# Compact 64x64 diagonal blocks and 64-row products in the triangular inverse of a two-block transformer kernel

## The chip, the cores and the metric

The kernel runs on one core of one Trainium2 chip (trn2). Time is device microseconds of one launch. TensorE is called PE in the profile (its weight loads PEld), VectorE DVE, ScalarE ACT, GpSimd POOL and SyncE SP. Everything is computed in fp32; a large product is made of three products of a high and a low part (types fp32r), a small one is a plain fp32 product, which shows as two weight loads and two matmuls.

## The reference

The reference is two transformer blocks over 256 tokens of width 1024. The first has three kinds of attention and a feed-forward layer; the second has a feed-forward layer, a mixer and another feed-forward layer. The change lies in the mixer, in its gated delta branch:

```python
A = jnp.where(strict, jnp.einsum('bhntk,bhnsk->bhnts', kb, k) * Lmat, 0.0)
T = lax.linalg.triangular_solve(eye + A, jnp.broadcast_to(eye, A.shape),
                                left_side=True, lower=True, unit_diagonal=True)
u = jnp.matmul(T, v * beta[..., None])
w = jnp.matmul(T, kb * jnp.exp(gam)[..., None])
```

`T` is the inverse of a unit lower triangular matrix. The kernel works on chunks of 128 tokens, so for every key head there are four 128x128 inverses: two chunks (`i` or `b`) times two value heads (`e`).

## The kernel before

Each engine runs its own program, written out by hand, and the engines meet only at semaphores. The part that matters is the loop over eight key heads of the mixer: `head(0, True, False)`, then `head(i, True, True)` for i = 1 to 7, then `head(8, False, True)`. In pass `i` the large product of head `i` (`gemm`) and the small work of head `i - 1` (`main`) are woven together. On PE the large product is cut into 24 quarters (`quarter(n)`) of 12 matmuls each, and between them stand the small products. Pass 8 has no large product; a few products of a later layer (`early_yh`, placed by the table `EARLY`) stand there as filler.

The inverse is built by doubling. `xi` holds the transposed inverse and `yi` the inverse, each 128 rows by 4 matrices of 128 columns; `nt` holds the negated strictly lower part. `yi` starts as the identity with the 1-wide level filled in (L1586, L1599), and `xi` is its transpose (L2245 on PE, L920 on ACT, which makes `t_ready`). For levels l = 1 to 6:

- `inv_t(l - 1)` (L2149, not for l = 1) transposes `xi` into PSUM with four matmuls, and `y_copy` on ACT (L826) takes the new half of the columns into `yi`.
- `inv_z(l)` multiplies `nt` by half of the columns of `xi`: four products, 128 rows deep and 64 columns wide, by `four` (L2118). `z_copy` on ACT (L813) takes the result into `zi`.
- one quarter, and often a product of the other branch (`level`, L2110, L2108, L2103, whose operands DVE makes in `decayed`, L1425 and L1426, and whose result it takes in `scored`, L1435 to L1442).
- `inv_w(l)` multiplies `yi` by `zi`: again four products by `four` (L2118).
- another quarter, and again perhaps a `level`. Meanwhile `inverse(l)` on DVE (L1455; for level 6 L1460) copies the result under a mask into `xi`; semaphore `xx_ready` releases the next `inv_t` and `inv_z`.

After level 6, `yi` multiplies the values (L2171, then the small chain L1533, L2189, L1545, L2195, L1551, L2207). Later in the pass PE makes the key products of the next head (L2234, semaphore `kq_done`), DVE makes `nt` from them (L1595), `mt` (L1597), the start of `yi` (L1599), two more scalings (L1601), then scans, copies and `w_low(4)`, and goes on into the next pass without a branch in between that matters.

DVE and ACT also prepare the weights of the large product in the same in-order queues. ACT's `split` (L556) takes 1.9 us for each piece of weights and DVE's `w_low` (L960) 2.3 us. `split` waits for PE to finish with the slot. All of this stands in one fixed order on each engine.

PSUM bank use in the inverse: `inv_z` writes bank 3 of `M`, `inv_w` bank 4 (level 6: bank 5), `inv_t` bank 5, `level` bank 0. In pass 8 `early_yh` uses bank 2 of `M` from part 14 on.

Of the kernel before, what the change touches and what calls it, by code (L numbers as in the profile page):

```python
# [13 lines left out]
P = 128  # L14
T = 256
# [67 lines left out]
def emit(nc, ctx, a, out):  # L83
# [132 lines left out]
    zi = grid(mix(4 * P), i=TT, e=2, c=P)  # L216
    vn0, vn1 = (grid(mix(2 * P), e=2, c=P) for _ in range(2))
# [21 lines left out]
    def x_half(i, h):  # L239
        return M[:, 2 * i + h, :].rearrange("p (k t) -> p k t", t=P)  # L240

    def yh_bank(tile):
# [61 lines left out]
    zz_done, zc_ready, ww_done, wt_done, xx_ready, yy_ready, yt_done = (  # L304
        sem(n) for n in ("zz_done", "zc_ready", "ww_done", "wt_done", "xx_ready", "yy_ready", "yt_done"))
# [235 lines left out]
    def _(act):  # L541
# [243 lines left out]
        def head(i, gemm, main):  # L785
# [23 lines left out]
            def z_copy(l):  # L809
                if not main:  # L810
                    return
                act.wait_ge(zz_done, l + (i - 1) * 6)
                nc.scalar.activation(halved(zi.rearrange("p i e c -> p (i e c)"), l, 0), packed(M[:, 3, 0:T], l),  # L813
                                     ACT.Copy).then_inc(zc_ready, 1)
# [7 lines left out]
            def y_copy(l):  # L822
                if not main:
                    return
                act.wait_ge(yt_done, l + (i - 1) * 5)
                nc.scalar.activation(halved(yi.rearrange("p i e c -> p (i e c)"), l, 1), halved(M[:, 5, :], l, 1),  # L826
                                     ACT.Copy).then_inc(yy_ready, 1)

            level_exp(1)
            z_copy(1)  # L830
            if not gemm:
                o_hi(0, GH - 1)
# [13 lines left out]
            z_copy(5)  # L846
            split_j(1)
# [70 lines left out]
            if gemm:  # L918
                act.wait_ge(t_done, i + 1)
                nc.scalar.activation(xi, M[:, 4, :].rearrange("p (i e c) -> p i e c", i=TT, e=2), ACT.Copy).then_inc(t_ready, 1)  # L920
# [32 lines left out]
    def _(dve):  # L953
# [420 lines left out]
        def head(i, gemm, main):  # L1374
# [72 lines left out]
            def inverse(l):  # L1447
                if not main:
                    return
                sz = 1 << l  # L1450
                shape = [P, 4, HD // sz, sz]
                if l < LEVELS - 1:
                    dve.wait_ge(ww_done, l + (i - 1) * 5)
                    dve.sem_inc(waited, 1)
                    v.copy_predicated(halved4(xi, l, 0), halved(lmask_t[:, l, :].bitcast(I32), l, 0).unsqueeze(1).to_broadcast(shape),  # L1455
                                      packed(M[:, 4, 0:T], l).rearrange("p (x n) s -> p x n s", x=4)).then_inc(xx_ready, 1)
                else:
                    dve.wait_ge(wt_done, i)
                    dve.sem_inc(waited, 1)
                    v.copy_predicated(halved4(yi, l, 1), halved(lmask[:, l, :].bitcast(I32), l, 1).unsqueeze(1).to_broadcast(shape),  # L1460
                                      packed(M[:, 5, 0:T], l).rearrange("p (x n) s -> p x n s", x=4)).then_inc(yy_ready, 1)
# [128 lines left out]
            if gemm:  # L1590
                dve.wait_ge(kq_done, i + 1)
                kk = M[:, 2, 0:3 * P].rearrange("p (b c) -> p b c", b=3)
                for e in range(2):
                    for b in range(TT):
                        v.scalar_tensor_tensor(out=nt[:, b, e, :], in0=kk[:, 2 * b, :], scalar=nbst[:, b, e:e + 1],  # L1595
                                               in1=lt[:, e, 2 * P * b:2 * P * b + P], op0=ALU.mult, op1=ALU.mult)
                v.tensor_tensor(mt, kk[:, 1, :].unsqueeze(1).to_broadcast([P, 2, P]), lt[:, :, P:T], ALU.mult)  # L1597
                settle()
                v.copy_predicated(yi, lmask[:, 0, :].bitcast(I32).unsqueeze(1).unsqueeze(1).to_broadcast([P, TT, 2, P]), nt)  # L1599
# [67 lines left out]
    def _(pe):  # L1667
# [397 lines left out]
        def early_yh(n):  # L2065
# [6 lines left out]
        EARLY = {2: (0, 2), 3: (2, 4), 4: (4, 6), 5: (6, 8), 6: (8, 10), 7: (10, 12), 8: (12, 14), 9: (14, 16),  # L2072
                 10: (16, 18), 11: (18, 19), 12: (19, 20), 13: (20, 21)}

        def head(i, gemm, main):
# [38 lines left out]
            def four(out_bank, lhs, rhs, l, side, done):  # L2114
                for b in range(TT):
                    for e in range(2):
                        at = P * b + HD * e
                        ins = mm(packed(M[:, out_bank, at:at + HD], l), lhs[:, b, e, :], halved(rhs[:, b, e, :], l, side),  # L2118
                                 start=True, stop=True)
                ins.then_inc(done, 1)  # L2120

            def inv_z(l):
# [6 lines left out]
                four(3, nt, xi, l, 0, zz_done)  # L2129

            def inv_w(l):
                if not main:
                    return
                pe.wait_ge(zc_ready, l + (i - 1) * 6)
                if l > 1:
                    pe.wait_ge(yy_ready, l - 1 + (i - 1) * 6)
                if l < LEVELS - 1:
                    four(4, yi, zi, l, 0, ww_done)
                else:
                    four(5, zi, yi, l, 1, wt_done)  # L2140

            def inv_t(l):
                if not main or l == 0:
                    return
                pe.wait_ge(xx_ready, l + (i - 1) * 5)
# [7 lines left out]
            for l in range(1, LEVELS):  # L2153
                inv_t(l - 1)
                inv_z(l)
                quarter(2 * l - 2)
# [11 lines left out]
            if main:  # L2168
                pe.wait_ge(yy_ready, i * 6)
# [148 lines left out]
```

## Time and profile before

| | us |
|---|---|
| median of 3 runs (1525.44 to 1526.99) | 1525.87 |
| the profiled execution | 1524.43 |
| its span, first to last instruction | 1522.7 |

| engine | busy us | share of span | instructions |
|---|---|---|---|
| PE | 1481.0 | 97% | 11072 |
| PEld | 1395.2 | 92% | 11072 |
| DVE | 1009.1 | 66% | 1559 |
| ACT | 716.4 | 47% | 960 |
| POOL | 28.7 | 2% | 73 |

The passes 1 to 8 of the head loop lie between about 765 and 1232 us. A busy PE is not a PE at its peak: matmuls overlap, so the length of one record is longer than the distance to the next, and costs have to be read from the distances of starts. DMA moves 148 GB/s on average and is busy half the time. Nothing in the head loop waits for weights to arrive.

### The profile page before, as it was taken

To read this page: it belongs to the slowest core of one execution; us is meant where nothing else is said; L and a number is where in the kernel's file an instruction comes from. 1 tells how busy PE (TensorE), PEld (TensorE's weight loads), DVE (VectorE), ACT (ScalarE), POOL (GpSimd) and SP (SyncE) were. 2 spreads that over 40 slices of the span, in tenths; PEclk is the share of its full clock that TensorE was granted. 3 is DMA by queue.
4 is the path that set the end of the run, shared out by engine and by line. 5 is a ranking of instruction groups with operands and counts; after the bars stand their busy time and mean duration, and the time that the engine had idled before them with its cause. 6 is when DMAs were issued, how large, how long until landed. Compare 5 with 4: busy or idle time off the path is not lost.

```text
span 1522.7 us, 28790 instructions
## 1 busy us (share of the span) xinstructions
PE 1481.0 (97%) x11072; PEld 1395.2 (92%) x11072; DVE 1009.1 (66%) x1559; ACT 716.4 (47%) x960; POOL 28.7 (2%) x73
## 2 busy tenths in 40 slices
PE   8999999999999999999999999999999999999998
PEld 8999999978999799998899999999999899799997
DVE  5786667674555755456888788787787755555544
ACT  4444444644444543445436546455464453444443
POOL 6000000000000000000000000000000000000000
PEclk9999999999999999999999999999999899999999
DMA  8454444555556456654643343443442325566661
GB/s 264 140 167 138 133 127 131 194 189 188 180 189 203 143 177 194 193 174 133 182 114 91 94 125 83 110 110 85 108 105 88 111 72 181 163 194 193 180 194 68
DMA packets 304640, 224.94 MB, mean 148 GB/s; under 512 B 10418, under 2 KB 288068, under 8 KB 304580
## 3 DMA queue, kind: packets, MB, share of 16 engines
q1 hardware_dynamic: 304580, 224.09, 49.5%
q8 instruction: 44, 0.72, 0.2%
q14 instruction: 16, 0.13, 0.0%
HBM read 223.02 MB, written 1.05 MB: 147 GB/s over the span
## 4 chain that ended last, share of the span: by engine, by line
PE 76%; DVE 13%; DVEq 4%; ACT 4%; issue 2%; DMA 0%; ACTq 0%
PE G L1674 15%; PE G L1676 14%; PE G L1675 14%; PE M L1679 5%; PE M L1680 5%; PE M L1681 5%; PE M L2118 4%; DVEq L957 4%; DVE w_lo L960 3%; PE M L1674 2%; PE M L1676 2%; PE M L1675 2%; ACT w_hi L556 2%; PE M L2149 1%; PE M L2110 1%
## 5 line engine op out<-in xcount | busy, mean ns | idle before, releaser
L960 DVE TENSOR_TENSOR w_lo<-w_raw,w_hi 128x2048 fp32r<-128x2048 f32 (+1 forms) x208 | 475.3, 2286 | 241.3 <-ACT w_hi L556 240.1
L1674 PE MATMUL G<-xa_hi,w_hi 128*128 128x256 f32 x2152 | 630.4, 293 | 0.9 <-DVE w_lo L960 0.5
L1675 PE MATMUL G<-xa_lo,w_hi 128*128 128x256 f32 x2152 | 608.8, 283 | 0.0
L1676 PE MATMUL G<-xa_hi,w_lo 128*128 128x256 f32 x2152 | 608.8, 283 | 0.0
L556 ACT ACTIVATE w_hi<-w_raw 128x2048 fp32r<-128x2048 f32 x207 | 395.0, 1908 | 288.4 <-PE G L1676 186.1
L1674 PEld LDWEIGHTS G<-xa_hi,w_hi 128*128 128x128 f32 x2152 | 411.9, 191 | 9.1 <-issue 7.5
L1675 PEld LDWEIGHTS G<-xa_lo,w_hi 128*128 128x128 f32 x2152 | 412.1, 191 | 6.0 <-issue 4.9
L1676 PEld LDWEIGHTS G<-xa_hi,w_lo 128*128 128x128 f32 x2152 | 411.4, 191 | 0.1
L1679 PE MATMUL M<-w_hi,xb_hi 128*128 128x512 f32 x304 | 118.9, 391 | 0.9 <-DVE xb_lo L960 0.9
L1680 PE MATMUL M<-w_lo,xb_hi 128*128 128x512 f32 x304 | 118.7, 390 | 0.0
L1681 PE MATMUL M<-w_hi,xb_lo 128*128 128x512 f32 x304 | 118.3, 389 | 0.0
L2118 PE MATMUL M<-arena 128*128 128x64 f32 x768 | 101.5, 275 | 1.5 <-ACT arena L813 1.4
L2118 PEld LDWEIGHTS M<-arena 128*128 128x128 f32 x768 | 96.1, 196 | 3.0 <-ACT arena L813 3.0
L731 ACT ACTIVATE arena<-G 128x256 f32<-128x256 f32 x44 | 16.9, 384 | 140.7 <-PE G L1676 140.7
L1679 PEld LDWEIGHTS M<-w_hi,xb_hi 128*128 128x128 f32 x304 | 57.2, 188 | 12.2 <-issue 1.4
L1681 PEld LDWEIGHTS M<-w_hi,xb_lo 128*128 128x128 f32 x304 | 57.1, 188 | 12.3
L1680 PEld LDWEIGHTS M<-w_lo,xb_hi 128*128 128x128 f32 x304 | 57.2, 188 | 10.6
L960 DVE TENSOR_TENSOR xb_lo<-arena,xb_hi 128x256 fp32r<-128x256 f32 (+2 forms) x68 | 35.3, 519 | 34.5 <-ACT xb_hi L733 21.2
L1291 DVE TENSOR_TENSOR arena<-arena,G 128x256 f32<-128x256 f32 x44 | 18.5, 421 | 56.7 <-ACT arena L731 56.7
L826 ACT ACTIVATE arena<-M 128x256 f32<-128x256 f32 x40 | 15.7, 392 | 85.2 <-PE M L2149 85.2
L1455 DVE COPY_PREDICATED arena<-lmask_t,M 128x256 f32<-128x256 int32 x40 | 24.4, 611 | 34.6 <-PE M L2118 32.7
L1384 DVE SCALAR_TENSOR_TENSOR arena<-arena 128x256 f32<-128x256 f32 x96 | 42.0, 479 | 2.2
(352 smaller groups left out, 2002.9 us busy)
## 6 DMA issues: line engine op xcount, KB each, us to landing
w_raw<-in_w_in SPq DMA_DIRECT2D x166, 512.0 KB, 4.5
w_raw<-in_ffn_w_in SPq DMA_DIRECT2D x88, 512.0 KB, 4.9
w_raw<-in_w_ff SPq DMA_DIRECT2D x64, 512.0 KB, 4.2
w_raw<-in_ffn_w_out SPq DMA_DIRECT2D x44, 512.0 KB, 4.0
w_raw<-in_w_out SPq DMA_DIRECT2D x16, 512.0 KB, 4.2
w_raw<-in_w_branch_gdn SPq DMA_DIRECT2D x16, 512.0 KB, 5.1
w_raw<-in_w_branch SPq DMA_DIRECT2D x12, 512.0 KB, 4.3
w_raw<-in_w_branch_hgrn SPq DMA_DIRECT2D x8, 512.0 KB, 3.9
```

The lines of the kernel that those rows point to most:

```text
L556: nc.scalar.activation(w_hi[:, slot, :], w_raw[:, slot, :], ACT.Copy).then_inc(hi_ready, 1)
L957: v.drain()
L960: return v.tensor_tensor(dst, src, hi.bitcast(F32), ALU.subtract)
L1384: ins = v.scalar_tensor_tensor(out=acc[:, n, :], in0=x, scalar=w, in1=acc[:, n, :], op0=ALU.mult, op1=ALU.add)
L1455: v.copy_predicated(halved4(xi, l, 0), halved(lmask_t[:, l, :].bitcast(I32), l, 0).unsqueeze(1).to_broadcast(shape), packed(M[:, 4, 0:T], ...
L1674: mm(out_, w[0], x[0], start=first, stop=False)
L1675: mm(out_, w[0], x[1], start=False, stop=False)
L1676: return mm(out_, w[1], x[0], start=False, stop=last_)
L1679: mm(out_, x[0], w[0], start=first, stop=False)
L1680: mm(out_, x[0], w[1], start=False, stop=False)
L1681: return mm(out_, x[1], w[0], start=False, stop=last_)
L2118: ins = mm(packed(M[:, out_bank, at:at + HD], l), lhs[:, b, e, :], halved(rhs[:, b, e, :], l, side), start=True, stop=True)
```

## The change

The level loop keeps the 64x64 diagonal blocks in compact form until level 5. A new tile `xc` holds, on its lower 64 partitions, the upper left block of each of the four transposed inverses, and on its upper 64 partitions the lower right block; so it is 256 columns wide instead of 512. `yc` and `zc` are compact views of the memory of `yi` and `zi`. `ntq` is a view of `nt` in another column order, so that the 64 columns of a block of both value heads lie side by side.

- `inv_z(l)` for l = 1 to 5 makes four products of 64 rows, one for each chunk and each half of the array (partitions 0 to 63 and 64 to 127), with 128 weight columns and 64 moving columns. The two halves write banks 3 and 4.
- `inv_w(l)` for l = 1 to 5 makes four products of 64 rows, one for each chunk and value head, again alternating between the halves. They write banks 1, 2, 3 and 4, 64 columns each.
- For level 6 both are four products of 64 rows, 64 weight columns and 64 moving columns, all on the same quarter of the array.
- `inv_t(l)` for l = 0 to 4 is two transposes of 128x128 instead of four; `inv_t(0)` is new and stands behind `inv_z(1)`. `inv_t(5)` is four as before.
- ACT has a new `y_copy(0)` of 256 columns behind `z_copy(1)`; `y_copy` copies 128 columns for l = 1 to 4 and 512 for l = 5. `spread` is new: two copies of 64 partitions take `xc` into `xi` behind `z_copy(5)` (semaphore `xf_ready`, awaited by DVE's `inverse(5)`). The copy L920 becomes two copies of 64 partitions.
- DVE's `inverse(l)` for l = 1 to 5 is two masked copies of 64 partitions and 128 columns instead of one of 128 partitions and 256 columns. For level 6 it is an unmasked copy of 64 partitions. Two memsets of 64 partitions stand ahead of the wait for `kq_done`, and the masked copy that starts `yi` is cut in two.
- `EARLY` moves filler in pass 8 from quarters 8 and 9 to quarters 10 to 12.

Its core:

```diff
+    xc = grid(mix(2 * P), i=TT, e=2, c=HD)
+    ntq = nt.rearrange("p i e c -> p (i e c)").rearrange("p (i h e c) -> p i h e c", i=TT, h=2, e=2)
+    yc = grid(yi.rearrange("p i e c -> p (i e c)")[:, 0:2 * P], i=TT, c=P)
+    zc = grid(zi.rearrange("p i e c -> p (i e c)")[:, 0:2 * P], h=2, i=TT, e=2, s=HD // 2)
...
+            def spread():
+                if not main:
+                    return
+                act.wait_ge(xx_ready, 4 + (i - 1) * 5)
+                for side in range(2):
+                    ins = nc.scalar.activation(quad(xi, side), xc[HD * side:HD * side + HD, :, :, :], ACT.Copy)
+                ins.then_inc(xf_ready, 1)
...
-                    v.copy_predicated(halved4(xi, l, 0), halved(lmask_t[:, l, :].bitcast(I32), l, 0).unsqueeze(1).to_broadcast(shape),
-                                      packed(M[:, 4, 0:T], l).rearrange("p (x n) s -> p x n s", x=4)).then_inc(xx_ready, 1)
+                    for side in range(2):
+                        own = slice(HD * side, HD * side + HD)
+                        new = M[own, 1:5, 32 * side:32 * side + 32].rearrange("p x (n s) -> p x n s", s=sz)
...
+                        ins = v.copy_predicated(old, halved(lmask_t[own, l, own].bitcast(I32), l, 0).unsqueeze(1)
+                                                .to_broadcast([HD, 4, 32 // sz, sz]), new)
+                    ins.then_inc(xx_ready, 1)
...
+                settle()
+                for side in range(2):
+                    v.memset(xi[HD * side:HD * side + HD, :, :, HD - HD * side:P - HD * side], 0.0)
                 dve.wait_ge(kq_done, i + 1)
...
-                four(3, nt, xi, l, 0, zz_done)
+                for b in range(TT):
+                    for side in range(2):
+                        if l == LEVELS - 1:
+                            ins = mm(M[HD:P, 3, P * b + HD * side:P * b + HD * side + HD], ntq[0:HD, b, 1, side, :],
+                                     xi[0:HD, b, side, 0:HD], start=True, stop=True)
+                        else:
+                            own = slice(HD * side, HD * side + HD)
+                            x = xc[own, b, :, :].rearrange("p e (n h s) -> p (e n) h s", h=2, s=1 << l)[:, :, 0, :]
+                            ins = mm(packed(M[:, 3 + side, HD * b:HD * b + HD], l),
+                                     ntq[own, b, side, :, :].rearrange("p e c -> p (e c)"), x, start=True, stop=True)
+                ins.then_inc(zz_done, 1)
...
+                            own = slice(HD * e, HD * e + HD)
+                            ins = mm(M[:, 1 + 2 * b + e, 0:HD].rearrange("p (h s) -> p h s", h=2), yc[own, b, :],
+                                     zc[own, :, b, e, :], start=True, stop=True)
...
+                if l < LEVELS - 2:
+                    for b in range(TT):
+                        ins = nc.tensor.transpose(M[:, 5, P * b:P * b + P], xc[:, b, :, :].rearrange("p e c -> p (e c)"), ident[:])
+                    ins.then_inc(yt_done, 1)
                     return
```

## Rows read from the trace of the kernel before

**Rows 1.** The page's part 4, the chain that ended last, by engine.
```profile
PE 76%; DVE 13%; DVEq 4%; ACT 4%; issue 2%; DMA 0%; ACTq 0%
```

**Rows 2.** Busy time by stretch: passes 1 to 7, then pass 8.
```profile
core 0: us, PE busy (x) PEld busy (x) DVE busy (x) ACT busy (x) POOL busy (x), PEclk, DMA share, GB/s
764.80:1196.40 431.60, 425.00 (x3472) 411.32 (x3471) 351.53 (x776) 226.71 (x399) 0.00 (x0) 1.00 0.38 102
1196.40:1232.00 35.60, 31.83 (x229) 31.11 (x228) 19.43 (x45) 15.16 (x35) 0.00 (x0) 0.81 0.21 60
```

**Rows 3.** Waits of passes 1 to 7: who for whom, us in total, times, longest.
```profile
PEld M L2195 <- DVE arena L1545: 4.8, 7, 0.7
...
PE M L2149 <- DVE arena L1455: 1.9, 6, 0.3
...
PEld M L2118 <- ACT arena L813: 1.4, 7, 0.3
```

**Rows 4.** PE in order of time, one product group alone: start, us, line, count.
```profile
785.00 0.28 PE L1676 MATMUL G<-xa_hi,w_lo 128*128 128x256 f32 x1
785.12 1.00 PE L2118 MATMUL M<-arena 128*128 128x64 f32 x8
785.93 0.36 PE L1674 MATMUL G<-xa_hi,w_hi 128*128 128x256 f32 x1
786.14 0.28 PE L1675 MATMUL G<-xa_lo,w_hi 128*128 128x256 f32 x1
```

**Rows 5.** PE in order of time around a 64-row group of the first block.
```profile
102.84 0.28 PE L1676 MATMUL G<-xa_hi,w_lo 128*128 128x256 f32 x1
103.05 0.50 PE L1839 MATMUL M<-arena 64*128 64x128 f32 x4
103.38 0.61 PE L1840 MATMUL M<-arena 64*128 64x256 f32 x4
103.92 0.38 PE L1679 MATMUL G<-w_hi,xa_hi 128*128 128x256 f32 x1
104.14 0.28 PE L1680 MATMUL G<-w_lo,xa_hi 128*128 128x256 f32 x1
```

**Rows 6.** Groups of weight loads by line and shape: busy us, mean ns, idle before.
```profile
L2118 PEld LDWEIGHTS M<-arena 128*128 128x128 f32 x768 | 96.1, 196 | 3.0 <-ACT arena L813 3.0
...
L1839 PEld LDWEIGHTS M<-arena 64*128 64x128 f32 x32 | 2.5, 184 | 1.0
```

**Rows 7.** PE in order of time around four transposes.
```profile
1009.41 0.28 PE L1676 MATMUL G<-xa_hi,w_lo 128*128 128x256 f32 x1
1009.53 0.60 PE L2245 MATMUL M<-ident,arena 128*128 128x128 f32 x4
...
1010.09 0.28 PE L1675 MATMUL G<-xa_lo,w_hi 128*128 128x256 f32 x1
```

**Rows 8.** DVE in order of time, pass 5: levels 1 and 3 of the inverse.
```profile
1017.05 0.72 DVE L1455 COPY_PREDICATED arena<-lmask_t,M 128x256 f32<-128x256 int32 x1
1017.58 0.32 DVE L1425 TENSOR_TENSOR arena<-arena 128x128 f32<-128x128 f32 x1
...
1025.57 2.29 DVE L960 TENSOR_TENSOR w_lo<-w_raw,w_hi 128x2048 fp32r<-128x2048 f32 x1 [0.54 <-ACT w_hi L556]
...
1028.75 0.59 DVE L1455 COPY_PREDICATED arena<-lmask_t,M 128x256 f32<-128x256 int32 x1 [0.28 <-issue]
```

**Rows 9.** DVE in order of time: level 5 of pass 5, and what follows it.
```profile
1039.29 0.49 DVE L1455 COPY_PREDICATED arena<-lmask_t,M 128x256 f32<-128x256 int32 x1 [2.50 <-PE M L2118]
...
1053.93 0.35 DVE L1551 TENSOR_SCALAR arena<-M,arena 128x128 f32<-128x128 f32 x1 [0.81 <-PE M L2195]
```

**Rows 10.** The two masked copies by line: ns min, median, max.
```profile
L1455 DVE COPY_PREDICATED arena<-lmask_t,M x40: 486/588/740, 769.4 to 1225.2; 128x256 f32<-128x256 int32 x40
...
L1442 DVE COPY_PREDICATED arena<-lmask,M x56: 284/294/447, 771.1 to 1228.5; 128x128 f32<-128x128 int32 x56
```

**Rows 11.** DVE in order of time behind kq_done, pass 5.
```profile
1067.19 1.13 DVE L1595 SCALAR_TENSOR_TENSOR arena<-M,arena 128x128 f32<-128x128 f32 x4 [0.78 <-PE M L2235]
...
1068.72 0.75 DVE L1599 COPY_PREDICATED arena<-lmask,arena 128x512 f32<-128x512 int32 x1
1069.36 1.00 DVE L1601 SCALAR_TENSOR_TENSOR arena<-M,arena 128x384 f32<-128x384 f32 x2
```

**Rows 12.** ACT in order of time, pass 5: the copy of level 1 and what follows.
```profile
1014.11 0.39 ACT L813 ACTIVATE arena<-M 128x256 f32<-128x256 f32 x1
1014.38 0.31 ACT L806 ACTIVATE arena<-arena 128x128 f32<-128x128 f32 x1
```

More of the change, by code:

```diff
@@ L240, in x_half, with quad @@
         return M[:, 2 * i + h, :].rearrange("p (k t) -> p k t", t=P)
+    def quad(ap, side):
+        return ap[HD * side:HD * side + HD, :, :, HD * side:HD * side + HD]
     def yh_bank(tile):
@@ L846, in head @@
             z_copy(5)
+            spread()
             split_j(1)
@@ L2112, in level @@
                 ins.then_inc(lev_done, 1)
[L2114 to L2120, printed above, removed]
             def inv_z(l):
@@ L2134, in inv_w, with inv_t @@
                 pe.wait_ge(zc_ready, l + (i - 1) * 6)
[L2135 to L2138, printed above, removed]
-                else:
-                    four(5, zi, yi, l, 1, wt_done)
-            def inv_t(l):
-                if not main or l == 0:
+                pe.wait_ge(yy_ready, l + (i - 1) * 7)
+                if l == LEVELS - 1:
+                    pe.sem_inc(waited, 1)
+                for b in range(TT):
+                    for e in range(2):
+                        if l == LEVELS - 1:
+                            at = P * b + HD * e
+                            ins = mm(M[0:HD, 5, at:at + HD], zi[HD:P, b, e, 0:HD], yi[HD:P, b, e, HD:P], start=True, stop=True)
+                        else:
+                            own = slice(HD * e, HD * e + HD)
+                            ins = mm(M[:, 1 + 2 * b + e, 0:HD].rearrange("p (h s) -> p h s", h=2), yc[own, b, :],
+                                     zc[own, :, b, e, :], start=True, stop=True)
+                ins.then_inc(ww_done if l < LEVELS - 1 else wt_done, 1)
+            def inv_t(l):
+                if not main:
+                    return
+                if l == 0:
+                    pe.wait_ge(t_ready, i)
+                else:
+                    pe.wait_ge(xx_ready, l + (i - 1) * 5)
+                if l < LEVELS - 2:
+                    for b in range(TT):
+                        ins = nc.tensor.transpose(M[:, 5, P * b:P * b + P], xc[:, b, :, :].rearrange("p e c -> p (e c)"), ident[:])
+                    ins.then_inc(yt_done, 1)
                     return
-                pe.wait_ge(xx_ready, l + (i - 1) * 5)
                 for b in range(TT):
@@ L2153, in head @@
             for l in range(1, LEVELS):
-                inv_t(l - 1)
+                if l > 1:
+                    inv_t(l - 1)
                 inv_z(l)
+                if l == 1:
+                    inv_t(0)
                 quarter(2 * l - 2)
@@ L2168, in head @@
             if main:
[L2169 removed]
+                pe.wait_ge(yy_ready, i * 7)
                 for e in range(2):
```

58 lines of the change are left out of this document (41 added, 17 removed).

## The prediction

> **What bounds the kernel now.** I read the page first. The chain that ended last is PE for three quarters and DVE for most of the rest [rows 1], so PE sets the time, but not alone. Then the busy time by stretch: passes 1 to 7 take 431.6 us, 61.66 us each, and PE is busy for all but 6.6 us of them; in pass 8 the granted clock is 0.81, part of it at the lower level, 1.2 GHz [rows 2]. Then the waits of passes 1 to 7: PE's loads wait 0.7 us a pass for DVE's L1545, about 0.3 for L1455, and 0.2 for ACT's L813 [rows 3]. These are small, yet they tell that DVE is right behind PE in places. Last, the engines in order of time, for what each group costs and where DVE has no gap.
>
> DVE runs without a real gap through three stretches of a pass. (A) From `kq_done`, where it had waited 0.78 us for PE [rows 11], through `w_low`, to the masked copy of level 1, whose end releases `inv_t(1)` [rows 8]. (C) From PE's end of the first piece of weights, over ACT's split and DVE's `w_low` (which waits 0.54 us for the split), to the copy of level 3 [rows 8]. (F) From the end of PE's `inv_w(5)`, where DVE had waited 2.50 us, to L1545, after which PE's L2195 is what DVE waits for [rows 9]. What PE saves inside A, C or F is lost; what DVE gains in length there is paid in full. Between them PE is the bound.
>
> **Part 1, the products (L2118).** A group of four 128-row products alone: from the last matmul of the large product before it (785.00) to the second after it (786.14) 1.14 us; without a group these are two steps of 0.12, so the group costs 0.90, and read over many groups 0.89: eight weight loads at 0.111 [rows 4]. Moving 64 columns takes less than loading 128, so the loads set this.
>
> What 64-row products cost is shown in the first block [rows 5]: two products on each half of the array. 102.84 to 104.14 is 1.30, less 0.24: 1.06. Each half has two passes of 128 columns and two of 256, 0.11 and 0.22 each by their distances, 0.66 together. So both halves run side by side (one after the other would be 1.31 plus something), and 0.40 is spent on entering and leaving: the first load starts 0.21 after the last matmul instead of beside it, is not hidden, and the same again on the way out. The load of 64 rows takes 184 ns against 196 [rows 6]: the columns count, not the rows.
>
> The new group has four passes on each half, bound by loads: 4 x 0.11 = 0.44, plus 0.40 = 0.84; the last pass streams only 64 columns, 0.05 instead of 0.11, so about 0.79. I take 0.79, so 0.10 saved a group; at 0.85 it is 0.04. The level 6 groups have half the weight columns, eight passes one after the other; between 0.8 and 1.3 each, no row has them, but they lie in F and are covered by DVE there as long as they stay under about 1.0.
>
> The drain is also a rule of the Trainium skill, TensorEngine Tiling (Array Packing), Key Properties: changing the tiling mode drains TensorE. The trace agrees, with 0.40 us. The same page's table of theoretical speedups gives up to twice for a dimension of 64 or less; that would make the group 0.45, and it is the fourth rival.
>
> **Part 2, the transposes.** Four cost 1010.09 - 1009.41 - 0.24 = 0.44 [rows 7], two 0.22. `inv_t(1)` to `inv_t(4)` save 0.22 each; `inv_t(0)` adds 0.22 in A, where PE has about 0.5 us of waits to cover it.
>
> **Part 3, DVE.** The masked copy of level 1 lasts 0.72, and the next starts 0.53 after it [rows 8]; the five levels run from 0.74 down to 0.49 [rows 10]. No row has a DVE instruction on 64 partitions. The nearest is L1442, with the 128 columns that each half will have: 0.44 for short runs, 0.29 for long ones [rows 10]. Bounds: a half costs nothing more than half of the whole (sum 0), or as much as the whole. I take halves of 0.455, 0.37 and 0.33 for levels 1, 3 and 5, one behind the other with no overlap: +0.19, +0.15, +0.17. The copy that starts `yi`, 0.64 to the next start [rows 11], becomes two of 256 columns, about 0.38 each: +0.12. Level 6's copy on DVE gets simpler, -0.10. The two memsets and the drain before `kq_done` hide in DVE's wait of 0.78; without that cover they cost some 0.5. The copies of `nt` keep count and size: 0.
>
> **Part 4, ACT.** `y_copy(0)` stands behind `z_copy(1)`, and `inv_w(1)` now waits for both. A copy of this size takes 0.27 to the next start [rows 12], so `inv_w(1)` starts 0.27 later, but `inv_t(1)` behind it waits for DVE anyway (about 0.3, rows 3), and 0.10 + 0.10 come off the groups: 0. Behind `y_copy(0)` on ACT are queued two exponentials of 0.3, whose user is behind `w_low` on DVE. `spread` (two copies, some 0.7) delays the split behind it; DVE needs that split over a microsecond later: 0. The split copy at L920 adds under 0.1 and has 0.7 of slack: 0. `inverse(5)` waits for `xf_ready`, while its product is still a quarter (1.4 us) away: 0.
>
> **The sum for one pass of 1 to 7.** (Negative is earlier.)
> - A: `inv_t(1)` starts at +0.12 + 0.19 = +0.31.
> - Before the first piece ends: `inv_t(1)` -0.22, `inv_z(2)` and `inv_w(2)` -0.10 each: -0.11.
> - C: what PE saves on `inv_t(2)`, `inv_z(3)`, `inv_w(3)` waits for DVE; the copy of level 3 adds 0.15: +0.04 at `inv_t(3)`.
> - `inv_t(3)`, `inv_t(4)` and the groups z4, w4, z5, w5 between them: -0.44 - 0.40: -0.80 at the end of `inv_w(5)`.
> - F: +0.17 - 0.10: -0.73. Until the next `kq_done` nothing changes.
>
> Seven passes: -5.1. Pass 8 has no long DVE chain behind level 1; its first wait grows by 0.27 + 0.2, the transposes save 0.9 (more at the lower clock), the groups of levels 2 to 5 0.8, and moving the filler costs about 0.4: -1.0. In all -6.1. The profiled execution (1524.43, span 1522.7) would come to 1518.3; it lies 1.4 below the median, so the median goes from 1525.9 to **1519.8**.
>
> A measurement of this kernel can tell about 0.2%, 3.05 us, from no change: 1522.8 and 1528.9 are the borders.
>
> **Rivals.**
>
> (1) DVE holds back more. Neighbouring DVE instructions overlap by 0.2 (1017.05 + 0.72 against 1017.58, rows 8). If a change of half costs this overlap for the instruction behind each pair too, `w_low` behind level 5 starts 0.2 later, and the copies of levels 1 and 2 push `inv_t(2)` back by 0.5: the gain falls by 0.3 a pass, to -0.43. Seven passes -3.0, pass 8 -0.5: **1522.4**. For it: nothing in the trace, since all rows have 128 partitions; against it: the same. The Trainium skill, VectorE: DVE Perf Modes, section on two Vector instructions with no wait between them, has this rule: one that starts in another quarter of the partitions than the last waits until all before it have finished. No run here shows it. Chance 0.2.
>
> (2) The gain of a group is only 0.04 and DVE pays as I said: PE's gains on the path fall by 0.36 a pass (six groups), so -0.37 a pass, -2.5 in all, and pass 8 gives nothing: **1523.3**. Chance 0.14.
>
> (3) Slower: a masked copy of 64 partitions and half the columns costs as much as the whole one, because its cost is fixed. Then stretch A grows by 0.64 (L1599) and 0.52, C by 0.43, F by 0.37 - 0.10. Per pass 1.86 against the 1.25 that PE saves on the path: +0.6, seven passes +4.3, pass 8 -0.5: **1529.7**. It decides from 1.25 us of DVE growth on. Against it: L1442 has half the columns of L1455 and takes 0.29 against 0.59 by the medians [rows 10]. Chance 0.1.
>
> (4) Entering and leaving costs nothing: a group 0.45, another 0.34 on each of six groups a pass and twelve in pass 8: -14 - 4: **1501**. Against it: the 64-row group of rows 5 pays, as do the eleven of its kind in the first block. Chance 0.08.
>
> (5) The change does not do what it says: the halves do not run side by side. Then 8 x 0.11 + 0.40 = 1.28, +0.39 on 12 groups, less 0.67 and some 0.6 of waits: +3.4 a pass, eight passes: **1553**. Against it rows 5, though there each half had its two products in a row, while here they alternate. Chance 0.06.
>
> **How the numbers follow.** Forecast 0.42, rivals 0.2, 0.14, 0.1, 0.08, 0.06. The range 1509 to 1530 leaves out (4) and (5), 0.14, and a little at its ends; its low end is the forecast with DVE's halves at no extra cost (0.63 less in each of seven passes) , a better pass 8, and a step toward (4). Pass 8 adds 2 either way, since the clock level there can last longer or shorter. Faster by over 0.2%: most of the forecast, about half of (1), a third of (2), and (4): 0.60. Same: 0.24. Slower: 0.16.
>
> **What the profile after would show.** The pass at 60.9 us instead of 61.66. A new group 0.79 from the same reading as in rows 4, with two matmuls starting within 0.02 of each other. PE's wait at `inv_t(1)` grown to 0.5 or more, and the wait for L1545 as before. The pair of masked copies 0.9 us at level 1 and 0.66 at level 5. Wrong if a group costs under 0.6 or over 0.9, if the pairs of DVE take over 1.0, or if pass 8 spends another stretch at 1.2 GHz.

## The result and the profile after

| | before | after |
|---|---|---|
| median us | 1524.99 (7 runs) | 1530.19 (7 runs, 1528.94 to 1530.69) |
| profiled execution, span | 1524.43, 1522.7 | 1530.69, 1529.0 |
| period of passes 3 to 7 | 61.77 | 61.26 |
| start of pass 8 to a product behind level 6 | 33.96 | 43.31 |
| from there to the end | 292.0 | 292.0 |

The ratio is 1.0032, 95% interval [1.002, 1.0044]: the changed kernel is slower by 5.2 us. The forecast was 1519.8, so it has the wrong sign, and the time lies just above the range. The last three lines of the table are read in the trace from the start of the two `hvt` transposes (L2251 before, L2319 after) to the next such start, and to the second matmul of L2175 and L2243, which stand behind level 6. They say where it went: passes 1 to 7 gained 3.3 us (431.9 to 428.6), pass 8 lost 9.35, and nothing behind it moved.

The busy time of the changed kernel by stretch (columns as in rows 2), passes 1 to 7, then pass 8:

```profile
765.10:1193.70 428.60, 412.06 (x3433) 380.21 (x3432) 367.79 (x833) 235.20 (x427) 0.00 (x0) 1.00 0.38 103
1193.70:1237.00 43.30, 38.95 (x213) 34.53 (x212) 20.38 (x47) 16.35 (x38) 0.00 (x0) 0.54 0.17 49
```

Against rows 2 the passes are shorter although DVE is busy 16 us longer and PE idles more (16.5 us against 6.6). Pass 8 has fewer matmuls than before, yet takes longer at a granted clock of 0.54 instead of 0.81. Cut finer, the kernel before and then the one after:

```profile
1201.00:1214.00 13.00, 10.89 (x53) 10.71 (x52) 8.60 (x15) 2.87 (x10) 0.00 (x0) 0.50 0.55 154
1214.00:1230.00 16.00, 16.00 (x142) 15.87 (x142) 5.73 (x21) 6.21 (x18) 0.00 (x0) 1.00 0.00 1
```

```profile
1198.00:1214.00 16.00, 13.48 (x72) 11.81 (x71) 10.00 (x19) 3.77 (x13) 0.00 (x0) 0.50 0.44 123
1214.00:1238.00 24.00, 24.00 (x127) 21.64 (x125) 7.04 (x25) 8.46 (x19) 0.00 (x0) 0.50 0.00 1
```

In both, the clock falls to 0.5 (1.2 GHz) in the first waits of pass 8. Before, it is back at 1.0 (2.4 GHz) near 1214. After, it stays at 0.5 for 24 us more, with PE busy in all of them. PE in order of time shows these waits; the clock falls at or just behind the end of the first (near 1197.2 here, near 1200.3 before):

```profile
1194.83 0.61 PE L2154 MATMUL M<-arena 128*128 128x128 f32 x4
1197.27 1.12 PE L2195 MATMUL M<-arena 64*128 64x64 f32 x8 [1.83 <-ACT arena L838]
1198.32 1.11 PE L2156 MATMUL M<-arena 128*128 128x64 f32 x4
1201.96 0.48 PE L2208 MATMUL M<-ident,arena 128*128 128x128 f32 x1 [2.52 <-DVE arena L1493]
```

The same places of the kernel before:

```profile
1199.84 1.65 PE L2118 MATMUL M<-arena 128*128 128x64 f32 x8 [1.41 <-ACT arena L813]
1201.29 1.05 PE L2110 MATMUL M<-arena 128*128 128x64 f32 x4
1204.45 1.11 PE L2149 MATMUL M<-ident,arena 128*128 128x128 f32 x4 [2.11 <-DVE arena L1455]
```

Both waits are 0.4 us longer in the changed kernel.

In the passes, a group of 64-row products alone, as rows 4 showed for the old one:

```profile
1030.46 0.28 PE L1722 MATMUL G<-xa_hi,w_lo 128*128 128x256 f32 x1
1030.67 0.66 PE L2195 MATMUL M<-arena 64*128 64x64 f32 x8
1031.26 0.39 PE L1720 MATMUL G<-xa_hi,w_hi 128*128 128x256 f32 x1
1031.48 0.28 PE L1721 MATMUL G<-xa_lo,w_hi 128*128 128x256 f32 x1
```

1030.46 to 1031.48 is 1.02, less 0.24: 0.78, as forecast (0.79). The first matmul starts 0.21 after the last one of the large product, and the step behind the group is 0.22 instead of 0.12: entering and leaving are both there. DVE at level 1, to be set beside the first two lines of rows 8:

```profile
1015.59 0.89 DVE L1493 COPY_PREDICATED arena<-lmask_t,M 64x128 f32<-64x128 int32 x2
1016.51 0.30 DVE L1454 TENSOR_TENSOR arena<-arena 128x128 f32<-128x128 f32 x1
```

The next instruction starts 0.92 after the pair does; behind the one copy of rows 8 it was 0.53. Read one by one at level 1 (eight pairs), the first half lasts 0.42 to 0.44 us and the second 0.44 to 0.46; the second starts 0.44 after the first, and the next instruction 0.47 after the second: nothing overlaps. And the waits of PE's weight loads in passes 1 to 7 (us in total, times, longest), in the changed kernel and then before:

```profile
PEld M L2208 <- DVE arena L1493: 9.8, 13, 1.0
...
PEld M L2156 <- DVE arena L1471: 5.5, 7, 0.8
PEld M L2263 <- DVE arena L1583: 4.0, 7, 0.6
PEld M L2195 <- ACT arena L838: 3.7, 7, 0.6
```

```profile
PEld M L2195 <- DVE arena L1545: 4.8, 7, 0.7
...
PEld M L2110 <- DVE arena L1442: 2.7, 7, 0.4
PEld M L2149 <- DVE arena L1455: 2.7, 6, 0.5
PEld M L2118 <- ACT arena L813: 1.4, 7, 0.3
```

The wait for the masked copy has grown from 2.7 to 9.8 us, that for `scored` (L1442 before, L1471 now) from 2.7 to 5.5, and that for ACT ahead of `inv_w(1)` from 1.4 to 3.7: PE saves time and hands part of it back.

### The profile page after: what moved, and what is told of

Read it like the earlier page. It is cut to its first block, busy times and chain, and to the rows that moved or that the text cites. A ratio compares the mean times of both kernels' runs of the same rounds, so it can differ in the third digit from the quotient of the medians.

```text
span 1529.0 us, 28792 instructions
## 1 busy us (share of the span) xinstructions
PE 1478.4 (97%) x11024; PEld 1370.2 (90%) x11024; DVE 1027.6 (67%) x1623; ACT 726.2 (47%) x992; POOL 28.1 (2%) x73
## 4 chain that ended last, share of the span: by engine, by line
PE 70%; DVE 15%; ACT 6%; DVEq 5%; issue 3%; ACTq 1%; POOL 0%; POOLq 0%
PE G L1720 14%; PE G L1721 13%; PE G L1722 13%; DVE w_lo L989 5%; PE M L1725 5%; PE M L1726 5%; PE M L1727 5%; DVEq L986 4%; ACT w_hi L563 2%; PE M L1720 2%; PE M L1722 2%; PE M L1721 2%; PE M L2156 1%; PE M L2195 1%; PE M L2177 1%
## 5 line engine op out<-in xcount | busy, mean ns | idle before, releaser
L1493 DVE COPY_PREDICATED arena<-lmask_t,M 64x128 f32<-64x128 int32 x80 | 30.3, 379 | 24.5 <-PE M L2195 21.9
L840 ACT ACTIVATE arena<-M 128x128 f32<-128x128 f32 x32 | 9.0, 280 | 72.3 <-PE M L2208 72.3
L2156 PE MATMUL M<-arena 128*128 128x64 f32 x224 | 34.6, 280 | 4.1 <-DVE arena L1471 4.1
L2156 PEld LDWEIGHTS M<-arena 128*128 128x128 f32 x224 | 32.7, 208 | 5.6 <-DVE arena L1471 5.5
```

The costliest lines, as they stand in the source:

```text
L1493: ins = v.copy_predicated(old, halved(lmask_t[own, l, own].bitcast(I32), l, 0).unsqueeze(1) .to_broadcast([HD, 4, 32 // sz, sz]), new)
L2156: ins = mm(packed(M[:, 0, HD * b:HD * b + HD], l - 1), left[:, blk], halved(right[:, blk], l - 1, 1), start=True, stop=True)
```

## Experiments

Two questions: (H) what keeps the gain of a pass at 0.51 us instead of 0.73, and (C) what keeps the clock down in pass 8. All medians are of executions of one chip per batch, beside the kernel before on the same chip. "Pass" is the period of passes 3 to 7, "pass 8" the stretch of the table above; these two and the clock are those of the profiled execution, which in e8, e10 and e11 lies far from the median.

| run | median us | ratio to before, 95% | pass | pass 8 | its clock |
|---|---|---|---|---|---|
| before | 1523.8 to 1525.0 | | 61.77 | 33.96 | 0.80 |
| after | 1530.19 | 1.0032 [1.002, 1.0044] | 61.26 | 43.31 | 0.54 |
| e1_hybrid | 1524.36 | 0.9992 [0.9983, 1.0002] | 61.25 | 37.91 | 0.77 |
| e2_before_early | 1524.90 | 0.9999 [0.999, 1.0009] | 61.78 | 34.15 | 0.85 |
| e3_after_spin | 1528.74 | 1.0018 [1.0008, 1.0027] | 61.26 | 42.69 | 0.66 |
| e4_before_halves | 1531.57 | 1.004 [1.0025, 1.0054] | 62.58 | 34.84 | 0.80 |
| e5_after_spin3 | 1517.35 | 0.9956 [0.9939, 0.9972] | 61.26 | 30.53 | 1.00 |
| e6_before_spin3 | 1520.88 | 0.9981 [0.9971, 0.9991] | 61.80 | 31.28 | 1.00 |
| e7_before_wide | 1524.90 | 1.0005 [0.9995, 1.0015] | 61.83 | 34.30 | 0.80 |
| e8_before_edges | 1536.98 | 1.0086 [1.0069, 1.0103] | 61.79 | 39.58 | 0.83 |
| e10_before_edges2 | 1547.21 | 1.0168 [1.0121, 1.0215] | 61.80 | 45.36 | 0.85 |
| e11_edges_again | 1547.93 | 1.015 [1.0095, 1.0205] | 61.77 | 64.94 | 0.53 |
| e9_whole_spin3 | 1503.27 | 0.9863 [0.9847, 0.988] | 59.58 | 29.21 | 1.00 |
| e12_whole | 1516.44 | 0.9941 [0.9924, 0.9957] | 59.57 | 41.88 | 0.56 |

**e1_hybrid: passes 1 to 7 changed, pass 8 in the old form.** In pass 8 every part (ACT's and DVE's copies, PE's groups, the transposes) takes the branch of the kernel before; ACT first puts `nt` and `xc` into the old order.

```diff
             def inv_z(l):
...
+                if not gemm:
+                    if l == 1:
+                        pe.wait_ge(t_full, 1)
+                    else:
+                        pe.wait_ge(xx_ready, l - 1 + (i - 1) * 5)
+                    return four(3, of(gbc), of(xi), l, 0, zz_done)
```

> Passes 1 to 7 as in the changed kernel, pass 8 with the 128-row products, the four-matmul transposes and the single masked copies of the kernel before (with one rearranging copy of nt and the spreading of xc ahead, about 1 us more on ACT). The filler table is the changed one. Theory C (clock: the 64-row groups with their idle edges leave TensorE too little active in pass 8, so the granted clock, which falls in both kernels at its first waits, does not come back): the clock returns to 1.0 near the middle of pass 8, pass 8 takes 36 to 38 us instead of 45, total 1523 (1521.5 to 1525). Theory F (the moved filler keeps the clock low): clock stays at 0.5, total 1530 or more. Theory L (the lower clock is an accident of where the pass begins): the clock may stay low as well.

The periods are those of the changed kernel, the clock comes back at about 1215, and the loss is gone: 1524.36 against 1530.19. So it lies in the new form of pass 8: its products, its transposes or its copies, which this run changes together. The gain of the passes is not seen in the total, because pass 8 is 4 us longer than before with the reordering ahead of it (37.91 against 33.96).

**e2_before_early: the filler.** Only the new table `EARLY` in the kernel before.

```diff
-        EARLY = {2: (0, 2), 3: (2, 4), 4: (4, 6), 5: (6, 8), 6: (8, 10), 7: (10, 12), 8: (12, 14), 9: (14, 16),
-                 10: (16, 18), 11: (18, 19), 12: (19, 20), 13: (20, 21)}
+        EARLY = {2: (0, 2), 3: (2, 4), 4: (4, 6), 5: (6, 8), 6: (8, 10), 7: (10, 12), 8: (12, 13), 9: (13, 14),
+                 10: (14, 16), 11: (16, 18), 12: (18, 20), 13: (20, 21)}
```

> The kernel before with only the filler table of the change. Theory F: the clock stays at 0.5 to the end of pass 8 and the time goes to 1532 or so. Theories C and L: the clock comes back as before and the time is that of the kernel before plus at most 0.5 us.

Pass 8 grows by 0.2 us and the total not at all. The moved filler is not the cause. Nor is a longer wait by itself: PE's wait for the first masked copy is 2.78 us in this run, longer than the 2.52 of the changed kernel, the first wait of e1 is 3.73 against 1.83, and in both runs the clock comes back, near 1214 and 1215.

**e4_before_halves: DVE's halves alone.** The kernel before, with the masked copy of levels 1 to 5 as two copies of 64 partitions.

```diff
-                    v.copy_predicated(halved4(xi, l, 0), halved(lmask_t[:, l, :].bitcast(I32), l, 0).unsqueeze(1).to_broadcast(shape),
-                                      packed(M[:, 4, 0:T], l).rearrange("p (x n) s -> p x n s", x=4)).then_inc(xx_ready, 1)
+                    for side in range(2):
+                        own = slice(HD * side, HD * side + HD)
+                        ins = v.copy_predicated(
+                            halved4(xi, l, 0)[own, :, (32 // sz) * side:(32 // sz) * side + 32 // sz, :],
+                            halved(lmask_t[own, l, own].bitcast(I32), l, 0).unsqueeze(1).to_broadcast([HD, 4, 32 // sz, sz]),
+                            M[own, 4, 0:T].rearrange("p (x h n s) -> p x h n s", x=4, h=2, s=sz)[:, :, side, :, :])
+                    ins.then_inc(xx_ready, 1)
```

> The kernel before with DVE's part alone: the masked copy of levels 1 to 5 as two copies of 64 partitions and 128 columns; products, transposes and ACT as before. Theory H (a DVE instruction that starts at another partition than the last does not overlap it): the second starts 0.43 behind the first at level 1 and the next instruction again 0.45 behind, each pass grows by 0.3 (level 1) + 0.15 (level 3) + 0.35 (level 5 and the start of w_low) = about 0.8, total plus 5 to 7 us: 1531. Rival (the pair overlaps like others, 0.2): each pass plus 0.3, total 1527.

A pass grows from 61.77 to 62.58, by 0.82. All else being before's, this is the price of the halves alone. The changed kernel's pass is 1.32 shorter than this one, which is what the rest of the change brings (the forecast had 1.25). The halves stand in pass 8 too, and its clock comes back after some 13.6 us at 0.5, as in the kernel before: they are not what keeps it down. DVE at level 1 in this run (start, length):

```profile
1020.39 0.88 DVE L1457 COPY_PREDICATED arena<-lmask_t,M 64x128 f32<-64x128 int32 x2
1021.30 0.30 DVE L1425 TENSOR_TENSOR arena<-arena 128x128 f32<-128x128 f32 x1
```

**e7_before_wide: the same cut without a change of partitions.** Two copies of 128 columns again, but each on all 128 partitions. The edit is shown against e4; the mask changes in the same way.

```diff
-                            halved4(xi, l, 0)[own, :, (32 // sz) * side:(32 // sz) * side + 32 // sz, :],
+                            halved4(xi, l, 0)[:, :, (32 // sz) * side:(32 // sz) * side + 32 // sz, :],
...
-                            M[own, 4, 0:T].rearrange("p (x h n s) -> p x h n s", x=4, h=2, s=sz)[:, :, side, :, :])
+                            M[:, 4, 0:T].rearrange("p (x h n s) -> p x h n s", x=4, h=2, s=sz)[:, :, side, :, :])
```

> The kernel before, with DVE's masked copy of levels 1 to 5 cut into two of 128 partitions and 128 columns (by column halves), where the earlier run had two of 64 partitions and 128 columns. Columns and count are the same, only the partitions do not change. (H, what costs is that DVE does not overlap two instructions on different partitions) The second copy starts 0.2 us before the first ends, the next instruction too: a pass 62.0 to 62.2 us instead of 62.58, the kernel 1527 to 1529. (Rival, two instructions cost what they cost, with no part from the partitions) The pair starts 0.43 apart as before and the pass stays at 62.5 to 62.6, the kernel at 1531 to 1532.

```profile
1017.94 0.73 DVE L1456 COPY_PREDICATED arena<-lmask_t,M 128x128 f32<-128x128 int32 x2
1018.46 0.33 DVE L1425 TENSOR_TENSOR arena<-arena 128x128 f32<-128x128 f32 x1
```

The next instruction starts 0.52 after the pair, as behind one copy of 256 columns (0.53, rows 8). One by one: the second starts 0.23 after the first, though the first lasts 0.44, and the next 0.29 to 0.30 after the second. The pass is 61.83 against 61.77. So cutting a copy in two costs almost nothing, less than I expected; putting the parts on different partitions costs 0.75 us a pass. H holds, and its rival is refuted.

**e3_after_spin: idle products in the waits.** The changed kernel; in pass 8 PE computes products nobody reads, 512 columns each, two ahead of `inv_w(1)` and three ahead of `inv_t(1)`.

```diff
+        def warm(count):
+            pe.wait_ge(evac[1], EV_Y[1])
+            for _ in range(count):
+                mm(G[:, 1, :], ident[:], lmask[:, 0:4, :].rearrange("p l c -> p (l c)"), start=True, stop=True)
...
+                if l == 1 and not gemm:
+                    warm(WARM[0])
                 inv_w(l)
```

> The changed kernel with five idle 512-column products in pass 8, two ahead of the wait of inv_w(1) and three ahead of the wait of inv_t(1), into a free bank: extra work that no result needs. Theory C and theory L both say the clock need not fall: if it stays at 1.0, pass 8 takes 31 to 34 us instead of 45 and the time is 1517 to 1520. If the granted clock still falls or the 64-row groups pull it down later by themselves, theory C in its strong form (they can't even hold it) gives 1528 to 1532.

Only half a hit. 1528.74 is the time that the strong form of C forecast, but not for its reason: the clock is held through the first two waits and the 64-row groups behind them, and then falls in a third wait, that of `inv_t(2)`:

```profile
1205.49 0.28 PE L1722 MATMUL G<-xa_hi,w_lo 128*128 128x256 f32 x1
1207.74 0.69 PE L2215 MATMUL M<-ident,arena 128*128 128x128 f32 x2 [1.97 <-DVE arena L1493]
1208.36 1.12 PE L2184 MATMUL M<-arena 64*128 64x64 f32 x8
```

The same eight matmuls lasted 0.66 before this wait. From there it stays at 0.5 to the end of level 6, as in the changed kernel.

**e5_after_spin3: the third wait filled as well.**

```diff
-        WARM = (2, 3)
+        WARM = (2, 3, 2)
...
+                if l == 2 and not gemm:
+                    warm(WARM[2])
```

> The changed kernel with idle 512-column products in pass 8: two ahead of inv_w(1), three ahead of inv_t(1), two ahead of inv_t(2), in the waits for ACT and DVE. (C) The lower clock costs pass 8 its 9 us, and the wait at inv_t(2) was what let it fall with the five: the clock stays at 1.0 to the end of the inverse, pass 8 takes 32 to 34 us instead of 43.3, and the kernel 1519 to 1520.5. (C2) Groups of 64 rows bring the clock down whatever stands ahead of them: it falls again within the levels 2 to 5, pass 8 takes 40 to 43 us, and the kernel 1527 to 1530.

```profile
1205.78 1.88 PE L2124 MATMUL G<-lmask,ident 128*128 128x512 f32 x4
1207.91 0.44 PE L2215 MATMUL M<-ident,arena 128*128 128x128 f32 x2 [0.25 <-DVE arena L1493]
```

```profile
1193.80:1224.33 30.53, 29.10 (x228) 22.27 (x226) 20.18 (x48) 15.59 (x38) 0.00 (x0) 1.00 0.25 69
```

The clock is 1.00 throughout, pass 8 takes 30.53 us, less than I had expected, and the kernel 1517.35, where the changed kernel has 43.31 and 1530.19: some 12.8 us for seven idle products. C holds. C2 is refuted: 64-row groups do not bring the clock down. What this run, e3 and the changed kernel show together is that it does not come back among them once it is down.

**e6_before_spin3: the same seven products in the kernel before.** The edit is the same.

> The kernel before with the same seven idle products at the same places. (C and C2 alike) In 128-row form the clock is held at 1.0 throughout pass 8: some 1.5 to 3 us of the 34.0 of pass 8 go, 1522 to 1523.5. If the lower clock is no price at all in the kernel before, the idle products only add: 1525 to 1526.5. Set against the run with the seven in the changed kernel, this gives the worth of the change with the clock out of it: by the passes 1 to 7 alone -3.5 us.

1520.88; pass 8 is 2.7 us shorter. Against e5, with the clock at 1.0 in both, the change is worth 3.5 us by the medians. The traces show 3.5 in passes 1 to 7 and 0.75 in pass 8, 4.25 together; the profiled execution of e6, 1522.46, is one of its slower ones.

**e8_before_edges: entering and leaving alone.** In the kernel before, one small 64-row product ahead of each of the 128-row groups of pass 8 from level 2 on. These are ten groups, not the eight of the expectation.

```diff
             def four(out_bank, lhs, rhs, l, side, done):
+                if not gemm and l > 1:
+                    mm(M[:, 1, 0:HD], ident[0:HD, :], ident[0:HD, 0:HD], start=True, stop=True)
                 for b in range(TT):
```

> The kernel before, with one 64-row, 64-column product that nobody reads ahead of each 128-row group of pass 8 from level 2 on, so that PE enters and leaves the 64-row form as often as in the changed kernel, while the work stays 128-row. (E, entering and leaving, with the array empty for 0.4 us each time, is what keeps the clock down) The clock stays at 0.5 until the level 6 product or longer, pass 8 takes 42 us or more, the kernel 1533 or more. (W, it is the half array work in between that does) The clock comes back near 1214 as before, and pass 8 grows by eight times 0.4 to 0.6, to 37 to 39 us, the kernel 1528 to 1530.

The expectations divide the executions between them. The profiled one took 1528.97 us with the clock back near 1215, as W says. Four others took 1536.27 to 1537.21, as E says. No profile shows where their time went, but the granted clock over the whole execution is on record for each: 0.994 for the profiled one, 0.986 to 0.989 for the four.

**e10_before_edges2: two in each group.**

```diff
+                    edge()
                 for b in range(TT):
+                    if b and not gemm and l > 1:
+                        edge()
```

> The kernel before, with two of the 64-row, 64-column products in each group of pass 8 from level 2 on (ahead of it and in its middle) where the last run had one. That run came out at 1529 once, with the clock back at 1216, and at 1536 to 1537 four times. (E, entering and leaving the 64-row form keeps the clock down) With twice as many the clock stays at 0.5 until the product behind level 6 in all executions, pass 8 takes 45 us or more, the kernel 1538 to 1543. (W, only work on half the array does) The clock comes back near 1218 in the profile, pass 8 takes 42 to 43 us, the kernel 1532 to 1534.

Again divided: 1532.73 in the profiled execution (clock back near 1215, 0.995 over the whole), and 1540.80, 1553.62 and 1555.22 in the others (0.987, 0.979, 0.976: the longer, the lower). E had said all executions, which is a miss.

**e11_edges_again: the same kernel once more**, to see a long execution.

> The same kernel as in the last run of this kind (before, with two 64-row products in each group of pass 8): its profiled execution took 1533 us, with the clock back at 1215, while three others took 1541, 1554 and 1555, which no profile shows. (E) A profile of a longer execution shows the clock at 0.5 beyond 1220, to 1240 or more, and pass 8 longer by what is missing. (Rival: something outside pass 8 is longer in them) A longer execution with the clock back near 1215. If the execution is again one of 1533, it tells nothing.

This time the profiled execution was a long one, 1555.18 us:

```profile
1204.00:1214.00 10.00, 9.16 (x36) 8.00 (x37) 5.35 (x11) 1.70 (x6) 0.00 (x0) 0.50 0.45 122
1214.00:1224.00 10.00, 10.00 (x42) 8.98 (x41) 1.34 (x4) 1.18 (x4) 0.00 (x0) 0.50 0.00 0
1224.00:1262.00 38.00, 38.00 (x156) 34.29 (x156) 5.82 (x20) 7.52 (x17) 0.00 (x0) 0.50 0.00 1
1262.00:1272.00 10.00, 8.45 (x62) 7.71 (x62) 4.74 (x11) 4.21 (x6) 0.00 (x0) 1.00 0.00 0
```

The same stretches of the profiled execution of e10, which is the same program:

```profile
1204.00:1214.00 10.00, 10.00 (x41) 8.85 (x40) 4.56 (x8) 1.18 (x4) 0.00 (x0) 0.50 0.38 105
1214.00:1224.00 10.00, 10.00 (x68) 8.83 (x68) 2.11 (x9) 1.56 (x5) 0.00 (x0) 0.92 0.01 2
```

The 128-row work of the kernel before, with 20 tiny 64-row products added, can leave the clock at 0.5 until 1262, with PE busy in all of the 48 us from 1214 on. It comes back only behind the last of them. So E is possible, and by the times and clocks of nine of the eleven executions in these three runs it is usual, but it is not certain from one execution to the next. The changed kernel stayed low in every one of its 7 executions: 1528.94 to 1530.69 us, at a clock of 0.982 to 0.985 over the whole, where the kernel before has 0.992 to 0.995. Whether entering and leaving alone does that there, or the work on half the array as well, no run separates.

**e9_whole_spin3: the change without halves on DVE.** The blocks lie in a tile `xw` of 512 columns, each on the partitions where the 64-row products want it; the other partitions of its columns are never read. So DVE's copies run over all 128 partitions.

```diff
-    xc = grid(mix(2 * P), i=TT, e=2, c=HD)
+    xw = grid(mix(4 * P), h=2, i=TT, e=2, c=HD)
...
+                        for side in range(2):
+                            old = halved(xw[:, side, :, :, :].rearrange("p i e c -> p (i e c)"), l, 0)
+                            ins = v.copy_predicated(old.rearrange("p (x n) s -> p x n s", x=4),
+                                                    halved(lmask_t[:, l, HD * side:HD * side + HD].bitcast(I32), l, 0)
+                                                    .unsqueeze(1).to_broadcast([P, 4, 32 // sz, sz]),
+                                                    M[:, 1:5, 32 * side:32 * side + 32].rearrange("p x (n s) -> p x n s", s=sz))
...
-                        ins = nc.tensor.transpose(M[:, 5, P * b:P * b + P], xc[:, b, :, :].rearrange("p e c -> p (e c)"), ident[:])
+                        for side in range(2):
+                            own = slice(HD * side, HD * side + HD)
+                            ins = nc.tensor.transpose(M[:, 5 - 3 * side, HD * b:HD * b + HD],
+                                                      xw[own, side, b, :, :].rearrange("p e c -> p (e c)"), ident[own, own])
```

> The changed kernel with the seven idle products, and no DVE instruction of the levels on 64 partitions: the diagonal blocks lie in a tile of 512 columns, each on its own partitions, the masked copy of levels 1 to 4 is two of 128 partitions and 128 columns, that of level 5 one of 256, and the memsets are gone. For that inv_t of levels 0 to 4 becomes four 64-row transposes, two side by side, behind inv_z (at 0.11 each and two at a time the same 0.22 as now), y_copy two copies on ACT, spread two of 128 partitions. (H, the 0.82 us a pass that the halves on DVE cost come back, since only the change of partitions cost them) A pass 60.4 to 60.7 us instead of 61.26, that is the -1.3 of PE against 61.77 before; 7 passes -4 to -6 us, and the kernel 1511 to 1514 against 1517.4 with the spins alone. (Rival: DVE is not what holds the pass any more, or ACT's extra copies take its place) A pass 61.0 to 61.3, the kernel 1516 to 1518.

1503.27 us, 21 less than before: a miss to the good side. The pass is 59.58, that is 1.68 below the changed kernel's where 0.55 to 0.85 was expected. The waits of PE's loads in passes 1 to 7:

```profile
PEld M L2186 <- DVE arena L1496: 8.0, 20, 0.5
...
PEld M L2204 <- ACT arena L843: 3.5, 7, 0.5
...
PEld M L2165 <- DVE arena L1475: 2.3, 7, 0.3
```

The group that holds the longest wait for DVE's masked copy costs 1.27 us instead of 1.88, the one behind `level` in level 6 1.59 instead of 2.04, and the four 64-row transposes, joined to their 64-row group, 0.13 where two 128-row ones took 0.23. The first two differ mostly by the wait for DVE in them (0.66 to 0.29 us, and 0.58 to 0.13). Together with the group of `inv_t(1)` (2.04 to 1.72) they make most of the 1.7 us by which all small products of a pass, waits included, cost less (26.9 to 25.2, each read as in rows 4). The run also dropped the two memsets and the drain ahead of `kq_done` and reordered `inv_z` and `inv_t`, and `z_copy` and `y_copy` on ACT; how the 1.68 divides between these and the masked copies was not tried apart.

**e12_whole: the same without the seven idle products.**

> The kernel of the 1503 us, without the seven idle products of pass 8: diagonal blocks on their own partitions in 512 columns, full-partition DVE copies, 64-row transposes. (C) The clock falls in the first waits of pass 8 and the 64-row groups keep it at 0.5 until the product behind level 6: pass 8 takes 41 to 44 us instead of 29.2, the kernel 1514 to 1518. (Rival: with the transposes in 64-row form and fewer waits for DVE, the clock comes back within the levels) Pass 8 takes 32 to 37 us, the kernel 1506 to 1511.

Pass 8 takes 41.88 us at a clock of 0.56, the kernel 1516.44. C is met for the second time, in another program: holding the clock is worth 13.2 us here.

## Why the prediction was wrong

**The group, part 1: right.** 0.78 measured, 0.79 forecast, from the 0.40 of entering and leaving of rows 5. The two halves run side by side, so rivals 4 and 5 fall, and rival 2 with its 0.04 too.

**The transposes, part 2: right** within the reading: two cost 0.23 in a group.

**DVE, part 3: the durations right, the overlap not.** The halves last 0.43 and 0.44 at level 1 (0.455 forecast) and 0.31 and 0.32 at level 5 (0.33). But rival 1 is what happened: an instruction on other partitions than the last starts only when that one has ended. The Trainium skill, VectorE: DVE Perf Modes, section on two Vector instructions with no wait between them, says so, and the trace agrees with 0.44 against 0.23 us from start to start. Halves cost 0.82 a pass (e4), against the 0.51 of the forecast for levels 1, 3 and 5: the 0.3 that rival 1 priced. With it a pass was to gain 0.43, and gained 0.51. The step that failed is that the instruction behind a pair was still taken to overlap it by 0.2, with nothing in the trace for it; it starts 0.47 after a half of 0.44. The rule should have had the larger chance. The prediction also read rows 3 loosely: the 1.9 us for L1455 are waits of PE's matmuls, and its loads wait 2.7.

**ACT, part 4: not at nothing.** PE waits 0.5 us a pass for L838 (`y_copy(0)`), where it had waited 0.2 for ACT at this place; the wait stands ahead of a wait for DVE. That this later wait takes it up in the passes is argued, not shown; in pass 8 both waits are 0.4 us longer.

**Passes 1 to 7:** -5.1 forecast, -3.3 measured.

**Pass 8: the term that turned the sign.** -1.0 forecast, +9.35 measured. This is the step that failed for the kernel's time. The sum counted only work and the first wait: its transposes, its groups, the filler. That part was about right: with the clock at 1.0 in both forms the change takes 0.75 us off pass 8 (e6 against e5). It said that the clock level "can last longer or shorter" and gave it 2 us either way, with no row behind that number, and named another stretch at 1.2 GHz only as a sign of being wrong. The lower clock cost pass 8 12.8 us in the new form (43.31 against 30.53, e5) and 2.7 in the old (33.96 against 31.28, e6): 10.1 us more, less the 0.75 of work, are the 9.35. An estimate was to be had from the trace of before: the 16 us from 1214 to 1230 lie at 1.0, and a matmul step of the large products takes 0.21 us at 0.5, against 0.12:

```profile
1207.28 0.41 PE L1675 MATMUL G<-xa_lo,w_hi 128*128 128x256 f32 x1
1207.49 0.41 PE L1676 MATMUL G<-xa_hi,w_lo 128*128 128x256 f32 x1
```

If the lower level lasts to the end of level 6, these 16 us stretch to about 1.75 times, 28: some 12 us more. No rival had the lower clock as its mechanism. Rival 3 came near 1530 by another one, and it is refuted: a half lasts 0.44 us, where the whole copy lasts 0.72.

Had the clock come back as before, the forecast with rival 1 (1522.4) would have been near: 1524.99 less 3.3 in the passes is 1521.7.

## What to carry to other kernels

Where a stretch with short waits follows a dense one, look at the granted clock in it before a change there is priced: what must be bounded is how long the lower level can last, not only the work. Here idle products in waits of 1.4 to 2.5 us held the clock, and gave 2.7 us in one form of this stretch and about 13 in the other. And a tile that is laid out so that DVE keeps all its partitions can be worth more than a tile half the size: a pair of copies that also writes unused partitions takes 0.52 us to the next start (e9), a pair that changes partitions 0.92.

## What the runs showed of the hardware

- Once the granted clock was at 0.5, work in 64-row form, or 128-row work with tiny 64-row products in it, could stay there although PE was busy throughout: 24 us longer in the changed kernel, 48 us longer in one execution with 20 tiny products. At 1.0 the same groups do not bring it down (e5, e9). Why one execution of e10's program has the clock back at 1215 and another only at 1262 stays open.
- Two DVE copies of 128 partitions and 128 columns cost what one of 256 columns does (0.52 against 0.53 us to the next start), two of 64 partitions 0.92, all at level 1. ACT behaved alike: the second copy of `spread` (64 partitions each) started 0.418 us after a first that lasted 0.407, while with 128 partitions each (e9) it started 0.31 after a first that lasted 0.435.
- Four 64-row transposes beside a 64-row group cost 0.13 us, two 128-row ones 0.23.
